# Router of a routed mixture of experts: logit products inside the output loop, column sums on GpSimd, group counts ahead of the ranks

## What is computed

```python
for l in range(DEPTH):
    mix = even_mixer_2(x, ...) if l % 2 == 0 else odd_mixer(x, ...)      # ends in "@ w_o[l]"
    x = layer_norm_2(ALPHA * x + mix, ln_g[l, 0], ln_b[l, 0])
    ffn = routed_moe(x, router_w, router_b, moe_w_gate[l], moe_w_up[l], moe_w_down[l])
    x = layer_norm_2(ALPHA * x + ffn, ln_g[l, 1], ln_b[l, 1])
```

## Time and profile before

| | |
|---|---|
| time, median of 3 runs (lowest to highest) | 2371.82 us (2370.43 to 2372.3) |
| the profiled execution's own time | 2373.83 us |
| its span, first to last instruction | 2372.0 us |
| mean granted clock of PE | 0.972 |
| busy: PE, DVE, ACT, POOL | 2270.2, 1687.3, 1213.8, 274.1 us |
| share of the last-ending chain: PE, DVE, ACT | 72%, 15%, 9% |

### The profile page before, as it was taken

One profiled execution on the slowest core, in us unless ns is written; L12 is line 12 of the kernel. 1 busy time (PEld: TensorE's weight loads), 2 busy tenths in 40 slices (PEclk: granted clock), 3 DMA queues, 4 the chain that ended last, 5 costly groups with the idle time before them and its releaser, 6 DMA issues.

```text
span 2372.0 us, 33244 instructions
## 1 busy us (share of the span) xinstructions
PE 2270.2 (96%) x13716; PEld 1988.8 (84%) x13716; DVE 1687.3 (71%) x2348; ACT 1213.8 (51%) x1591; POOL 274.1 (12%) x324
## 2 busy tenths in 40 slices
PE   7999999899889999999999999989999989999997
PEld 3788888778779999998899998978888788888886
DVE  4786764534678888866666665558888876698886
ACT  2322222343654444455544444547777666577775
POOL 0011110120000000000000002327000111360000
PEclk9999999899999999999999999989999989899998
DMA  7556773222237787766444554329988722489884
GB/s 296 192 186 215 247 244 132 95 87 88 89 118 262 262 305 244 262 227 223 160 158 162 178 197 159 108 99 349 342 332 333 302 97 75 155 334 357 325 332 160
DMA packets 80819, 503.24 MB, mean 212 GB/s; under 512 B 9616, under 2 KB 10720, under 8 KB 28816
## 3 DMA queue, kind: packets, MB, share of 16 engines
q1 hardware_dynamic: 59120, 423.66, 48.6%
q0 software_dynamic: 21536, 77.33, 9.9%
HBM read 499.90 MB, written 1.05 MB: 211 GB/s over the span
## 4 chain that ended last, share of the span: by engine, by line
PE 72%; DVE 15%; ACT 9%; issue 3%; DMA 1%; DVEq 0%; SPq 0%; ACTq 0%
PE bank L440 70%; DVE wl L2127 7%; ACT wh L1436 6%; ACT s L1537 1%; DVE f L2335 1%; DVE s L2326 1%; DMA raw<-in_wmod 1%; PE bank L656 1%; PE bank L1312 1%; DVE rs L2180 0%; DVE hl L2310 0%; DVE tmpm L2303 0%; DVE X L2423 0%; ACT sq L1456 0%; DVE bank L2381 0%
## 5 line engine op out<-in xcount | busy, mean ns | idle before, releaser
L2127 DVE TENSOR_TENSOR wl<-raw,wh 128x2048 fp32r<-128x2048 f32 (+1 forms) x437 | 913.7, 2096 | 326.2 <-ACT wh L1436 322.6
L1436 ACT ACTIVATE wh<-raw 128x2048 fp32r<-128x2048 f32 (+1 forms) x437 | 756.9, 1739 | 309.7 <-PE bank L440 309.2
L440 PE MATMUL bank<-hh,wh 128*128 128x258 f32 (+2 forms) x2200 | 691.2, 314 | 28.9 <-DVE wl L2127 6.0
L440 PE MATMUL bank<-hh,wl 128*128 128x258 f32 (+2 forms) x2200 | 675.4, 307 | 0.0
L440 PE MATMUL bank<-hl,wh 128*128 128x258 f32 (+2 forms) x2200 | 673.8, 306 | 0.0
L440 PEld LDWEIGHTS bank<-hh,wh 128*128 128x128 f32 x2200 | 421.5, 192 | 61.1 <-issue 7.5
L440 PEld LDWEIGHTS bank<-hl,wh 128*128 128x128 f32 x2200 | 421.9, 192 | 18.7 <-issue 0.5
L440 PEld LDWEIGHTS bank<-hh,wl 128*128 128x128 f32 x2200 | 420.6, 191 | 19.0
L440 PE MATMUL bank<-wh,hh 128*128 128x512 f32 (+1 forms) x704 | 277.6, 394 | 3.3 <-DVE wl L2127 2.2
L440 PE MATMUL bank<-wl,hh 128*128 128x512 f32 (+1 forms) x704 | 274.2, 389 | 0.0
L440 PE MATMUL bank<-wh,hl 128*128 128x512 f32 (+1 forms) x704 | 274.0, 389 | 0.0
(11 more groups left out here) (495 smaller groups left out, 2647.3 us busy)
## 6 DMA issues: line engine op xcount, KB each, us to landing
raw<-in_wstream SPq DMA_DIRECT2D x393, 1024.0 KB, 4.9
mring<-in_wmodT POOLq DMA_DIRECT2D x128, 512.0 KB, 4.3
raw<-in_wmod SPq DMA_DIRECT2D x6, 1024.0 KB, 7.8
X<-in_xT SPq DMA_DIRECT2D x1, 2048.0 KB, 13.2
mods<-in_wmod SPq DMA_DIRECT2D x2, 1024.0 KB, 19.9
bias<-in_nabias POOLq DMA_DIRECT2D x16, 128.0 KB, 2.5
cB<-in_crow POOLq DMA_DIRECT2D x1, 1024.0 KB, 8.6
c_sglg<-in_sglg POOLq DMA_DIRECT2D x1, 1024.0 KB, 4.7
```

Of the source, the lines that this page charges most:

```text
L440: return e.matmul(out, lhsT, rhs, start=start, stop=stop, skip_group_check=True)
L1436: e.activation(wh[i % NB][:, o], raw[i % NR][:, o], ACT.Copy).then_inc(*slab_high(st.split + m))
L2127: e.tensor_tensor(wl[i % NB][:, o], raw[i % NR][:, o], wh[i % NB][:, o].bitcast(F32), ALU.subtract).then_inc(*slab_low(st.split + m))
```

## The change

The logits of a chunk become `token_logit`, three chunks of it behind the turns after d = 4 and three behind those after d = 6; the last two follow their chunk's turn in `token_last`. POOL adds the eight chunks of `wg` and of `wb` to one chunk each (`cs`, four dependent additions), and one product of `ones` with 32 columns replaces the 16 column-sum products, into a bank of the turned pieces. The counts get a bank of their own and are read first; the two triangle products become one of eight columns; DVE takes `most` and `flag` ahead of the ranks.

```diff
         def token_banks(l):
             for s_ in range(2):
                 claim(2 + s_, ("xt", l, s_, 0), act_out, "xt", l, s_, 0)
+            claim(4, ("aff", l), dve_out, "logit t", l, 1)
+
+        def column_sums(l):
+            b = banks[bank_of["xt", l, 0, 1]]
+            w.wait_ge(pool_out, "column sums", l)
+            mm(b[:, T:T + 32].rearrange("p (a x) -> p a x", a=2), ones[:], moes[l].cs[:, :, 0, :], True, True).then_inc(*result("c16", l))
...
-        def token_logits(l):
-            q = moes[l]
-            b = claim(7, ("c16", l), dve_out, "c16", l)
-            w.wait_ge(pool_out, "wb", l)
-            for half, m in enumerate((q.wg, q.wb)):
-                for d in range(KC):
-                    ins = mm(b[:, 16 * half:16 * half + 16], ones[:], m[:, d, :], d == 0 and half == 0, d == KC - 1)
-            ins.then_inc(*result("c16", l))
-            token_turn(l, KC - 2)
-            b = claim(4, ("aff", l), dve_out, "logit t", l, 1)
-            for d in range(KC):
-                if d == KC - 2:
-                    token_turn(l, KC - 1)
-                for s_ in range(2):
-                    ins = mm(b[:, 16 * s_:16 * s_ + 16], X[:, d, P * s_:P * s_ + P], q.wg[:, d, :], d == 0 and s_ == 0, d == KC - 1)
-            ins.then_inc(*result("aff", l))
+        def token_logit(l, d):
+            b = banks[bank_of["aff", l]]
+            w.wait_ge(dve_out, f"wo{l}", d)
+            w.wait_ge(pool_out, "wg", l)
+            for s_ in range(2):
+                ins = mm(b[:, 16 * s_:16 * s_ + 16], X[:, d, P * s_:P * s_ + P], moes[l].wg[:, d, :], d == 0 and s_ == 0, d == KC - 1)
+            ins.then_inc(*result("aff", l, d))
+
+        def token_last(l):
+            for d in (KC - 2, KC - 1):
+                token_turn(l, d)
+                token_logit(l, d)
...
                 if d in (2, 4, 6):
                     token_turn(0, d - 2)
                     token_turn(0, d - 1)
+                    if d == 6:
+                        column_sums(0)
+                    for i in range(3) if d == 4 else range(3, 6) if d == 6 else ():
+                        token_logit(0, i)
             result.mark("h read", "wo0")
-            token_logits(0)
+            token_last(0)
...
-            mm(b[:, 8:12], ones[:], one[:, 0, :], True, False)
-            mm(b[:, 8:12], ones[:], one[:, 1, :], False, True)
-            mm(b[:, 0:4], q.tri[:], one[:, 0, :], True, True)
-            mm(b[:, 4:8], q.tri[:], one[:, 1, :], True, False)
+            c = claim(4, ("count", l), dve_out, "moe", l, "most")
+            mm(c[:, 0:4], ones[:], one[:, 0, :], True, False)
+            mm(c[:, 0:4], ones[:], one[:, 1, :], False, True).then_inc(*result("count", l))
+            mm(b[:, 0:8], q.tri[:], q.gs[:, 1, :], True, False)
             mm(b[:, 4:8], ones[:], one[:, 0, :], False, True).then_inc(*result("rank", l))
...
-            w.wait_ge(result, "rank", l)
-            behind()
-            step(e.tensor_copy(q.rank[:], b[:, 0:8].rearrange("p (q g) -> p q g", q=2)), "rank")
-            behind()
-            step(e.tensor_reduce(q.most[:], b[0:1, 8:12], AX.X, ALU.max), "most")
+            w.wait_ge(result, "count", l)
+            step(e.tensor_reduce(q.most[:], banks[bank_of["count", l]][0:1, 0:4], AX.X, ALU.max), "most")
             behind()
             e.tensor_scalar(q.flag[:], q.most[:], 128.0, None, ALU.is_gt).then_inc(*dve_out("flag", l))
+            w.wait_ge(result, "rank", l)
+            step(e.tensor_copy(q.rank[:], b[:, 0:8].rearrange("p (q g) -> p q g", q=2)), "rank")
...
+            for half, m in enumerate((q.wg, q.wb)):
+                w.wait_ge(pool_out)
+                e.tensor_tensor(q.cs[:, half, :, :], m[:, 0:4, :], m[:, 4:8, :], ALU.add).then_inc(*pool_out("column sums", l))
+            for n in (2, 1):
+                w.wait_ge(pool_out)
+                e.tensor_tensor(q.cs[:, :, 0:n, :], q.cs[:, :, 0:n, :], q.cs[:, :, n:2 * n, :], ALU.add).then_inc(*pool_out("column sums", l))
```

More of the change, by code:

```diff
@@ L343, in moe_room @@
             q.c16 = sb(ph, f"c16{l}", [P, 2, 16])
+            q.cs = sb(ph, f"mcs{l}", [P, 2, 4, 16])
             q.lt = sb(ph, f"mlt{l}", [P, 2, 16])
@@ L1226, in odd_mixer @@
                     token_turn(1, d - 1)
+                    if d == 6:
+                        column_sums(1)
+                    for i in range(3) if d == 4 else range(3, 6) if d == 6 else ():
+                        token_logit(1, i)
             result.mark("h read", "wo1")
-            token_logits(1)
+            token_last(1)
             st.kept.difference_update((0, 1, 5, 6, 7))
@@ L1234, in moe @@
             one = q.gs[:, 1, :].rearrange("p (q g) -> p q g", q=2)
-            b = claim(7, ("rank", l), dve_out, "flag", l)
+            b = claim(7, ("rank", l), dve_out, "moe", l, "rank")
             w.wait_ge(dve_out, "moe", l, "group")
             w.wait_ge(const_in[f"tri{l}"], 0)
-            mm(b[:, 8:12], ones[:], one[:, 0, :], True, False)
-            mm(b[:, 8:12], ones[:], one[:, 1, :], False, True)
-            mm(b[:, 0:4], q.tri[:], one[:, 0, :], True, True)
-            mm(b[:, 4:8], q.tri[:], one[:, 1, :], True, False)
+            c = claim(4, ("count", l), dve_out, "moe", l, "most")
+            mm(c[:, 0:4], ones[:], one[:, 0, :], True, False)
+            mm(c[:, 0:4], ones[:], one[:, 1, :], False, True).then_inc(*result("count", l))
+            mm(b[:, 0:8], q.tri[:], q.gs[:, 1, :], True, False)
             mm(b[:, 4:8], ones[:], one[:, 0, :], False, True).then_inc(*result("rank", l))
@@ L3038, in moe @@
             e.tensor_scalar(q.rt[:, 0:2], q.mv[:, :, 1], 1e-5, None, ALU.add).then_inc(*dve_out("mean", nm))
-            c = banks[bank_of["c16", l]]
+            c = banks[bank_of["xt", l, 0, 1]]
             w.wait_ge(result, "c16", l)
-            e.tensor_scalar(q.c16[:, 0, :], c[:, 0:16], -1.0, None, ALU.mult).then_inc(*dve_out("c16", l))
-            e.tensor_copy(q.c16[:, 1, :], c[:, 16:32]).then_inc(*dve_out("c16", l))
-            w.wait_ge(result, "aff", l)
+            e.tensor_scalar(q.c16[:, 0, :], c[:, T:T + 16], -1.0, None, ALU.mult).then_inc(*dve_out("c16", l))
+            e.tensor_copy(q.c16[:, 1, :], c[:, T + 16:T + 32]).then_inc(*dve_out("c16", l))
+            w.wait_ge(result, "aff", l, KC - 1)
             behind()
```

## The result

The changed kernel took 2357.03 us (median of 4 runs, 2356.47 to 2359.96), the kernel before 2371.49 on the same chip; the ratio is 0.9942, 95% interval 0.9927 to 0.9957. It is faster, as forecast, but the gain is 14.5 us where the prediction had 9.6, and the time lies 2.0 us under the low end of the range. Repeated twice more among the experiments, the changed kernel has 15 runs in all with a median of 2358.70 (2355.86 to 2363.95); 76 runs of the kernel before had 2370.78 (2364.78 to 2375.45); one more run of it, of 4423.74 us, is left out. That difference, 12.1 us, is the better figure to explain. About 2.4 of the first 14.5 was a lucky draw; the median of 2358.70 still lies 0.3 us under the range.

A forecast was written before the change was run, and what follows sets the result against it. PE was taken to bound the experts, with the routing before them a pure delay. Gains of 4.55 + 3.23 + 0.99 + 0.82 = 9.6 us off 2371.82 gave 2362.2 us, range 2359 to 2367.

The forecast's parts named there:

- The loop: Output loop: 13 added products, 26 records, cost 2.9 us with switches at full clock.
- The rival: Granted clock falls inside the output loop: 2368.4 us, or 2375 if from the first burst; chance 0.17.
- What is late next: Behind the loop: chunk 6's transposes wait for chunk 7's residual; last statistics gain 4.55 us (block 0), 3.23 (block 1).
- the hand-over from the residual: Between chunk 7's residual and PE's restart: an allowance of 0.06 us, PE restarting at L + 0.67.
- POOL's additions: Ahead of the column sums: four additions, 0.40 to 0.7 us each, hidden; POOL late as rival, chance 0.03.
- Counts, flag, ranks: Behind the choice of groups: `Pm` starts 0.82 us earlier; gains of 0.99 and 0.82 us to the gather.
- The longer full clock: Rival: counts and ranks at full clock shrink by about 0.8 us in each block, 2360.6 us; chance 0.06.
- Nothing gives it back later: After the routing: the whole gain stays, since the experts' PE is full and the buffers are full when they start.
- the sum at two places: Up to the last statistics 4.55 and 3.23 us, counts to gather 0.99 and 0.82: 9.6 us.
- the rivals: Falling clock in the loop 0.17, longer full clock 0.06, experts bound by their stream 0.04, POOL late 0.03.

The follow-up runs named there:

- e6_after: The changed kernel, unchanged, run again for a third profile; 2359.18 us, ratio 0.9956.
- two late kernels: The changed kernel with one DVE operation of the first norm repeated three and four times, so that all that follows comes later; 2361.12 and 2364.97 us.
- e7_banks: Changed kernel with chunks 6 and 7 turned into banks 0 and 7, column sums beside the logits, finished pieces' statistics ahead of the last residual; 2357.64 us.
- e15_later3_after: The changed kernel with one DVE operation of the first norm repeated three times, all that follows about 2.1 us later; 2361.12 us.
- e3_loop: The kernel before with only the first part of the change, logits in the output loop and column sums on POOL; 2362.18 us.
- e9_both: e7_banks with ten idle products behind the last logits; 2355.86 us, ratio 0.9933.
- e12_warm10: The changed kernel with ten idle products behind the last logits, banks as they are; 2357.48 us, ratio 0.9944.
- e5_before: The kernel before, unchanged, run again for another profile; 2370.63 us, ratio 0.9997.
- e13_later1_before: The kernel before with one DVE operation of the first norm repeated once, all that follows about 0.7 us later; 2370.77 us.
- e16_later4_after: The changed kernel with one DVE operation of the first norm repeated four times, all that follows about 2.8 us later; 2364.97 us.
- four late kernels: One DVE operation of the first norm repeated: kernel before by one and two, changed kernel by three and four; 2370.77, 2371.65, 2361.12, 2364.97 us.

## Why the prediction was wrong, step by step

- **The loop.** 26 records with their switches at the full clock, 2.9 us forecast, 2.88 measured, granted clock 1.00. Right; the clock did fall there in 3 of 11 profiles with the new loop (`e6_after` and two late kernels), for 1.3 us in block 0. The rival's chance of 0.17 was fair, its price of up to 13 us was not seen.
- **What is late next.** A wait for chunk 7's residual ahead of chunk 6's turn, as said: 0.60 and 0.61 us idle for some 0.7. PE restarts 0.76 us behind L (the last weight product, at 1557.01, holds PE for 0.12) where the forecast had 0.67: the hand-over from the residual took 0.15 us (1557.74 to 1557.89), not 0.06. The two logit products behind gave that back, 0.36 us for 0.44, so these two small misses cancel. DVE late in block 0, PE late in block 1, as said. Loop to statistics fell by 4.67 (16.89 to 12.22) and 3.23 us (18.42 to 15.19); forecast 4.55 and 3.23. `e7_banks` confirms the wait by removing it.
- **POOL's additions.** 0.40 to 0.7 us each by estimate, 0.32 measured, free: no row of PE waits for them.
- **Counts, flag, ranks.** From the choice of groups to `Pm` 3.21 to 2.40 and 3.20 to 2.40 us, 0.81 and 0.80 for 0.82; from `Pm` to the gather 0.17 and 0.01 for 0.17 and nothing. Right.
- **The longer full clock** did not happen by itself: the counts ran at the lower clock (0.50 from 1562 to 1571), because PE idles 5.44 us ahead of them. With ten idle products the rival's 0.8 us for each block became 0.55, which had to be bought.
- **The step that failed** is the last one, 2371.82 - 9.6 = 2362.2 us, with the sentence "Nothing gives it back later". It takes the sum at two places for the whole difference, and puts what an earlier arrival does to TensorE's clock in the unchanged work at nothing (its reason, full buffers and a busy PE, does not bear on the clock); its range holds only the allowances of those places and the rivals. Of the 12.1 us between the medians, 9.7 are those places, 0.6 the stretch from gather to experts, and about 1.8 lie in work that neither kernel changes. The miss of 5.2 us (2362.2 to 2357.03) is thus 2.5 of gain that the sum lacks, 1.0 of a median of before that stood high (2371.82 for 2370.78), and 1.7 of low first runs of the changed kernel (2357.03 for 2358.70).

**What stands in that 1.8 us.** By the profiles it lies between the blocks. Experts 0 to loop 1 took 433.29 and 433.62 us in the two profiles of the kernel before, and 430.89, 431.12 and 431.62 in the three of the changed kernel: 2.2 us in the mean. Some 1.7 of them are one burst of products, the squares' sums of the layer norm behind block 0's experts. Timeline of PE there in the kernel before, in the changed kernel, and in `e15_later3_after`.

```profile
1889.53 5.42 PE L440 MATMUL bank<-sq,ones 128*128 128x256 f32 x16 [0.96 <-ACT sq L1473]
```

```profile
1879.15 3.72 PE L441 MATMUL bank<-sq,ones 128*128 128x256 f32 x16 [0.97 <-ACT sq L1484]
```

```profile
1883.84 5.45 PE L441 MATMUL bank<-sq,ones 128*128 128x256 f32 x16 [0.96 <-ACT sq L1484]
```

Over the first 3 us of it the granted clock was 0.50 in the kernel before, 1.00 in the changed kernel, and 0.50 in `e15_later3_after`. The burst took 3.72 us in all three profiles of the changed kernel, 5.4 to 5.7 in all seven with the old loop, and 5.3 to 5.5 again in five others with the new one: `e3_loop`, `e9_both`, `e12_warm10` and the two late kernels. In the late ones the whole stretch is back at 433.47 and 433.23 us. So the new loop as such does not shorten it; a shift by a few us decides whether the burst meets the lower clock. The 0.6 us behind the gather go the same way in block 1: gather to experts took 7.03 us before and 6.61 in the changed kernel, and 7.05 and 7.06 in the late ones. The late kernels' times do not show this loss cleanly, because other stretches move too: in `e15_later3_after` experts 1 to the end took 317.18 us in place of 320.30.

The runs, of which each has its span and mean granted clock, agree in kind: 2369.0 us and 0.9734 over the 76 runs of before, 2356.9 us and 0.9779 over the 15 of the changed kernel. The time at the lower level is twice the span times what the clock lacks of 1: 126.0 and 104.2 us, 21.8 less. The routing accounts for about 18: its two stretches of 45 us lack 0.23 and 0.19 in `e5_before` and 0.11 twice in the changed kernel, 37.8 and 19.8 us at the lower level. Some 3.8 us at the lower level are left for unchanged stretches. Were PE the limit in all of them, half would be lost, 1.9 us; by the spread of the 76 runs (0.971 to 0.977, some 1.1 us of time for each 0.001 on a straight line through them) it is 0.9. This is an account from means, not a cause shown.

Shown is that such falls come and go with the moment (`e13_later1_before` to `e16_later4_after`). The Trainium skill ("TensorE: Matmul & The Clock Gate", section "What's actually happening") says that the gate judges TensorE's activity in windows that run on by themselves and do not start with the kernel, so that it is a matter of the moment what falls into one; the four late kernels agree, and so do `e5_before` and `e12_warm10` at 600.87 and 600.86 us. Less like a free start is that the fall near 603 us came in five of five undelayed profiles with the old loop and in none of nine with the new one. Why the undelayed programs repeat so well, and so why the balance favours the changed kernel by some 2 us, stays open.

## What to carry to other kernels

Read a gain off the chain at the place, from profiled instruction to profiled instruction; that came within 0.1 us in the first two profiles here. Then ask what the rest of the program may do by itself: compare two profiles of the same kernel, and widen the range by what they differ (here 3 us ahead of block 0), both ways. An earlier arrival shifts all that follows against the clock's falls, and may gain or lose in work that was not touched (here 1.7 us in one layer norm). When work leaves a serial tail, look at what it covered: the wait under it comes out, and moving a bank claim and the statistics ahead of it may be worth as much as a part of the change (1.9 us in the profile here).

## What was not expected of the hardware

The granted clock near 603 us, in a stretch where PE is busy 27.00 of 27 us, fell or held depending on a delay of 0.7 to 2.8 us at 40 us: four products of 512 columns took 3.60 us after the fall in the kernel before and 1.99 at full clock in the changed one. The same program, run again, came to block 0 3.2 us sooner. An unread product of 256 columns, plain fp32, takes 0.44 us at full clock (8.02 us for 18).
